# Score matmuls of a PEER layer: both parts of the activations in one wide pass

## The chip, the cores and the metric

One Trainium2 chip, one NeuronCore of it. The metric is the device time of one execution in microseconds: before the change the median of 3 runs is 2077.22 us (2074.89 to 2080.98). The rows below come from one profiled execution of 2076.17 us.

## The reference, cut to what matters

One transformer layer over 256 tokens of width 2048: a token mixer, a layer norm, and PEER channel mixing, which picks 16 experts per head (8 heads) out of 16384 and adds their outputs.

```
q = (xt @ w_pq).reshape(n_tok, 8, 2, 128)
scores = einsum('thcd,hckd->thck', q, sub_keys)
s_top, i_top = top_k(scores, 16)
cand = s_top[:, :, 0, :, None] + s_top[:, :, 1, None, :]      # 16 x 16 sums
best, pos = top_k(cand, 16)
expert_idx = ...;  gate = softmax(best)
u = take(expert_u, idx);  act = gelu(einsum('thkd,td->thk', u, xb))
v = take(expert_v, idx);  out = einsum('thk,thkd->td', gate * act, v)
x = layer_norm(alpha * x + out)
```

All is float32.

## The kernel before, in words

The kernel does not gather experts. It scores all 16384 experts against all tokens, applies Gelu, multiplies by a dense matrix of gates (zero where an expert isn't picked), and multiplies by all of expert_v.

A float32 product is made of three matmuls in fp32r: each operand is split into a high part (ScalarE copies it with rounding, `split_hi`) and a low part (the rest, by a subtraction, `split_lo`), and high x high, high x low and low x high are summed in PSUM (`three`, L399). `act_hi` and `act_lo` are the two parts of the activations, 16 row tiles of 256 tokens each.

The stages in order of time: the mixer's projections and heads (to about 500 us); the PEER query projection; from 564 us the **expert scores**, which the change touches; from about 1362 us the **values** (expert_v); the last layer norm.

The expert scores run over 128 tiles of 128 experts in 64 pairs. A pair has 8 steps q, four per tile (t = 0 for q 0 to 3, t = 1 for q 4 to 7), and a step has four row tiles (`score_pair`, L631). For every step:
- SyncE loads expert_u rows into `raw` (`u_half`), VectorE transposes two steps' worth at a time (`turn_u`, L1336), part A into `u_cols` in SBUF, part B into PSUM banks 4 to 7;
- ScalarE makes `split_hi` (`split_u`, L892); it waits until TensorE has freed the slot (four slots, `split_free`);
- GpSimd makes `split_lo` in part A (pairs 0 to 25, L1727), VectorE in part B (L1331);
- TensorE waits for `lo_ready`, and for the first step of a tile also for `score_free`, then does 4 x 3 matmuls of 256 columns, tile t into PSUM bank t.
When a tile is done, ScalarE's `gelu` (L898) reads it from PSUM and writes it to the tile's row of `wexp`, or, from tile LATE = 51 on, to the buffer `late`, which VectorE multiplies into a row that holds ones or gates (`late_tile`, L1440).

Beside the matmuls VectorE has other work, in an order written out by hand. Pairs 0 to 15 are the **search**: `rank_set` (L1395) finds the best 16 of a head's keys, with the four transpositions of the next pair between its steps. The **softmax start** (L1476) follows, then the **decode** (L1494), in 8 rounds that go with pairs 17 to 24 and do comparison, selection and sum in SBUF, again with the next pair's transpositions between. Pairs 28 to 59 are the **gate stage**: two groups of four tokens per pair, GpSimd (`distances`, `weigh`), ScalarE (`hot_rows`, L908), TensorE (`gates_after`, L656) and VectorE (`apply_gates`, L1446). Every engine works through its own list in order; semaphores join them, so a wait in one list holds all that stands behind it there. ScalarE's list in `u_pair` (L934) is: steps 4 to 7 of a pair, Gelu of its tile 0, steps 0 to 3 of the next pair, Gelu of tile 1.

## Time and profile before

| | us |
|---|---|
| runs, median of 3 | 2077.22 |
| profiled execution | 2076.17 |
| its span, first to last instruction | 2074.4 |
| TensorE busy | 2042.9 (98%) |
| VectorE busy | 1483.8 (72%) |
| ScalarE busy | 1130.9 (55%) |
| GpSimd busy | 546.5 (26%) |

The time outside the span is 1.8 us. Matmuls are pipelined: their busy times overlap, so the spacing of their starts is what tells their price. GpSimd's share is small over the span, but all of it lies between 200 and 1320 us.

### The profile page before, as it was taken

The numbers are of one execution on the slowest core, as the hardware profiler recorded it, in microseconds if no ns is written. First come the engines' busy times: TensorE is split into PE (matmuls) and PEld (weight loads), VectorE is DVE, ScalarE is ACT, GpSimd is POOL, SyncE is SP. The second block draws the span as 40 slices with busy tenths as digits, with TensorE's granted clock in tenths as the row PEclk, the third lists the DMA queues.
The fourth block names the chain that finished last, engine by engine and source line by source line (L and its number), as shares of the span: only waits on it lengthen the run. The fifth ranks groups of instructions, "written<-read, shape, count | busy, mean of one in ns | idle before, by whom it ended". The sixth has DMA issues, their size and how long they took to land.

```text
span 2074.4 us, 42390 instructions
## 1 busy us (share of the span) xinstructions
PE 2042.9 (98%) x12326; PEld 1827.3 (88%) x12326; DVE 1483.8 (72%) x2397; ACT 1130.9 (55%) x1956; POOL 546.5 (26%) x384
## 2 busy tenths in 40 slices
PE   8999999989999999999999999999999999999997
PEld 6888888778899999999999999987888888888886
DVE  4555776675588879799999999965555555555557
ACT  4455555445455555466666666555555555555553
POOL 0000330100189999944444444100000000000001
PEclk9999999999999999999999999999999999999999
DMA  7755554667586657555555555657755555555654
GB/s 246 228 173 172 172 164 141 229 166 206 162 203 184 182 157 194 169 163 156 159 159 156 159 156 158 172 192 227 214 193 193 192 194 192 195 192 192 193 193 152
DMA packets 254251, 378.48 MB, mean 182 GB/s; under 512 B 41859, under 2 KB 173059, under 8 KB 253571
## 3 DMA queue, kind: packets, MB, share of 16 engines
q1 hardware_dynamic: 254208, 377.98, 60.6%
q8 instruction: 21, 0.34, 0.1%
q14 instruction: 22, 0.16, 0.0%
HBM read 373.69 MB, written 4.19 MB: 182 GB/s over the span
## 4 chain that ended last, share of the span: by engine, by line
PE 82%; POOL 9%; DVE 3%; issue 3%; DMA 2%; SPq 1%; ACT 1%; POOLq 0%; DVEq 0%; ACTq 0%
PE ps L401 26%; PE ps L403 26%; PE ps L402 26%; POOL split_lo L1730 8%; PE ps L664 3%; DMA raw<-in_expert_v 1%; DVE split_lo L1070 1%; DMA raw<-in_w_out 0%; PE ps L396 0%; SPq L374 0%; ACT split_hi L740 0%; DMA x_nat<-in_x 0%; DVE end_lo L1596 0%; DVE stats L1606 0%; PE ps L611 0%
## 5 line engine op out<-in xcount | busy, mean ns | idle before, releaser
L1070 DVE TENSOR_TENSOR split_lo<-raw,split_hi 128x512 fp32r<-128x512 f32 x840 | 602.7, 720 | 493.7 <-ACT split_hi L740 492.6
L740 ACT ACTIVATE split_hi<-raw 128x512 fp32r<-128x512 f32 x840 | 528.9, 631 | 564.2 <-PE ps L403 547.4
L401 PE MATMUL ps<-act_hi,split_hi 128*128 128x256 f32 x2048 | 586.0, 286 | 0.8 <-POOL split_lo L1730 0.6
L403 PE MATMUL ps<-act_hi,split_lo 128*128 128x256 f32 x2048 | 579.3, 283 | 0.0
L402 PE MATMUL ps<-act_lo,split_hi 128*128 128x256 f32 x2048 | 579.3, 283 | 0.0
L401 PEld LDWEIGHTS ps<-act_hi,split_hi 128*128 128x128 f32 x2048 | 392.6, 192 | 2.6 <-POOL split_lo L1730 1.9
L402 PEld LDWEIGHTS ps<-act_lo,split_hi 128*128 128x128 f32 x2048 | 392.9, 192 | 0.0
L403 PEld LDWEIGHTS ps<-act_hi,split_lo 128*128 128x128 f32 x2048 | 392.6, 192 | 0.0
L401 PE MATMUL ps<-split_hi,whalf_hi 128*128 128x512 f32 x992 | 386.0, 389 | 1.4 <-DVE split_lo L1070 1.4
L402 PE MATMUL ps<-split_lo,whalf_hi 128*128 128x512 f32 x992 | 385.9, 389 | 0.0
L403 PE MATMUL ps<-split_hi,whalf_lo 128*128 128x512 f32 x992 | 385.9, 389 | 0.0
L1730 POOL TENSOR_TENSOR split_lo<-u_cols,split_hi 128x512 fp32r<-128x512 f32 x208 | 282.2, 1370 | 122.8 <-ACT split_hi L896 105.0
L401 PE MATMUL ps<-split_hi,act_hi 128*128 128x512 f32 x688 | 276.0, 401 | 6.0 <-DVE split_lo L1070 5.7
L896 ACT ACTIVATE split_hi<-ps 128x512 fp32r<-128x512 f32 x304 | 177.0, 593 | 173.4 <-PE ps L403 173.0
L403 PE MATMUL ps<-split_hi,act_lo 128*128 128x512 f32 x688 | 269.5, 392 | 0.0
L402 PE MATMUL ps<-split_lo,act_hi 128*128 128x512 f32 x688 | 269.0, 391 | 0.0
L1717 POOL TENSOR_TENSOR stats<-stats 128x1 f32<-128x1 f32 (+1 forms) x6 | 9.7, 1609 | 889.1 <-DVE stats L1612 749.1
L401 PEld LDWEIGHTS ps<-split_hi,whalf_hi 128*128 128x128 f32 x992 | 186.2, 188 | 40.5 <-DVE split_lo L1070 1.8
L403 PEld LDWEIGHTS ps<-split_hi,whalf_lo 128*128 128x128 f32 x992 | 186.2, 188 | 38.7
L402 PEld LDWEIGHTS ps<-split_lo,whalf_hi 128*128 128x128 f32 x992 | 186.2, 188 | 38.6
L1333 DVE TENSOR_TENSOR split_lo<-ps,split_hi 128x512 fp32r<-128x512 f32 x304 | 198.0, 678 | 25.6 <-ACT split_hi L896 20.4
L896 ACT ACTIVATE split_hi<-u_cols 128x512 fp32r<-128x512 f32 x208 | 131.2, 632 | 143.9 <-PE ps L403 142.6
(188 smaller groups left out, 2121.4 us busy)
## 6 DMA issues: line engine op xcount, KB each, us to landing
raw<-in_expert_u SPq DMA_DIRECT2D x1024, 128.0 KB, 2.9
raw<-in_expert_v SPq DMA_DIRECT2D x256, 512.0 KB, 4.7
raw<-in_w_in SPq DMA_DIRECT2D x112, 512.0 KB, 3.8
raw<-in_w_out SPq DMA_DIRECT2D x32, 512.0 KB, 3.9
raw<-in_w_pq SPq DMA_DIRECT2D x128, 128.0 KB, 2.9
cst<-in_tables SPq DMA_DIRECT2D x3, 768.0 KB, 5.3
x_nat<-in_x SPq DMA_DIRECT2D x4, 512.0 KB, 6.9
x_dram<-x_cols SPq DMA_DIRECT2D x1, 2048.0 KB, 8.0
```

The lines of the kernel that those rows point to most:

```text
L401: nc.tensor.matmul(acc, l_hi, r_hi, start=first, stop=False)
L402: nc.tensor.matmul(acc, l_hi, r_lo, start=False, stop=False)
L403: return nc.tensor.matmul(acc, l_lo, r_hi, start=False, stop=last)
L664: last = nc.tensor.matmul(ps[:, 2 + parity, i * P:(i + 1) * P], hot[:, parity, 1, i, :], hot[:, parity, 0, i, :], start=True, stop=True)
L740: nc.scalar.activation(split_hi[:, q % SPLITS, :], raw[:, q // 2, q % 2, :], ACT.Copy).then_inc(hi_ready, 1)
L896: nc.scalar.activation(split_hi[:, q % SPLITS, :], src, ACT.Copy).then_inc(hi_ready, 1)
L1070: vec.tensor_tensor(split_lo[:, q % SPLITS, :], raw[:, q // 2, q % 2, :], split_hi[:, q % SPLITS, :].bitcast(f32), ALU.subtract).then_inc( ...
L1333: vec.tensor_tensor(split_lo[:, q % SPLITS, :], ps[:, 4 + q % 4, :], split_hi[:, q % SPLITS, :].bitcast(f32), ALU.subtract).then_inc(lo_re ...
L1717: eng.tensor_tensor(stats[:, RSTD + first:RSTD + first + w], stats[:, VAR + first:VAR + first + w], stats[:, NHALF:NHALF + w], ALU.pow).th ...
L1730: eng.tensor_tensor(split_lo[:, q % SPLITS, :], u_cols[:, q // 2, q % 2, :], split_hi[:, q % SPLITS, :].bitcast(f32), ALU.subtract).then_i ...
```

## The change

`act_hi` and `act_lo` now lie side by side for each row tile (`act_both`). A step of the scores does four passes of 512 columns, `split_hi` against both parts at once, which wait for `hi_ready` alone, and then four of 256 columns, `split_lo` against `act_hi`, after `lo_ready` (in the last step of a tile one wide pass comes last). A tile's PSUM bank then holds two halves. ScalarE copies the second half to SBUF (`second_half_out`), VectorE adds it to the first half in PSUM (`add_halves`) and writes `wexp` or `late`, and ScalarE's Gelu now works there in place, later than before: for tile 0 after step 2 of the next pair, for tile 1 after step 6 of the next pair. In part A the tiles take four banks in turn; part B has two, as before. `late_tile` moves from VectorE to GpSimd. VectorE's sums stand at fixed places between the search's, the decode's and the splits' instructions. The loops of part A go over two pairs at a time. The core of the diff:

```diff
-        act_hi = at("act_hi", [KT, SEQ], f32r, A_HI)
-        act_lo = at("act_lo", [KT, SEQ], f32r, A_LO)
+        act_both = at("act_both", [KT, 2, SEQ], f32r, A_HI)
+        act_hi, act_lo = act_both[:, :, 0, :], act_both[:, :, 1, :]
+        halves = at("halves", [4, SEQ], f32, KEEP + 9216)
...
-            def score_pair(pair, after=None):
+            def score_pair(pair, after=None, parity=None):
+                first = 0 if parity is None else 2 * parity
+                def wide(bank, q, i):
+                    k = q % 4 * 4 + i
+                    return nc.tensor.matmul(ps[:, bank, :], split_hi[:, q % SPLITS, i * P:(i + 1) * P],
+                                            act_both[:, k, :, :].rearrange("p a t -> p (a t)"), start=k == 0,
+                                            stop=k == KT - 1)
                 for q in range(8):
-                    if q % 4 == 0:
-                        pe.wait_ge(score_free, pair * 2 + (q // 4 + 1))
+                    t, end = q // 4, q % 4 == 3
+                    if q % 4 == 0 and not (isinstance(pair, int) and pair < 2):
+                        pe.wait_ge(score_free, pair * 2 + (t + 1 if parity is None else t - 1))
+                    pe.wait_ge(hi_ready, pair * 8 + (Q_U + q + 1))
+                    wides = 3 if end else 4
+                    for i in range(wides):
+                        wide(first + t, q, i)
                     pe.wait_ge(lo_ready, pair * 8 + (Q_U + q + 1))
                     for i in range(4):
-                        last = three(ps[:, q // 4, 0:SEQ], split_hi[:, q % SPLITS, i * P:(i + 1) * P],
-                                     split_lo[:, q % SPLITS, i * P:(i + 1) * P], act_hi[:, q % 4 * 4 + i, :],
-                                     act_lo[:, q % 4 * 4 + i, :], q % 4 == 0 and i == 0, q % 4 == 3 and i == 3)
+                        k = q % 4 * 4 + i
+                        last = nc.tensor.matmul(ps[:, first + t, 0:SEQ], split_lo[:, q % SPLITS, i * P:(i + 1) * P],
+                                                act_hi[:, k, :], start=False, stop=False)
+                    if end:
+                        last = wide(first + t, q, 3)
...
+            def second_half_out(pair, t, parity=None):
+                bank = t if parity is None else 2 * parity + t
                 act.wait_ge(split_free, pair * 8 + (Q_U + SPLITS + 4 * t + 4))
-                if is_late:
+                if parity is None or isinstance(pair, int) and 2 * pair + t >= LATE:
                     act.wait_ge(late_used, pair * 2 + (t + 1 - LATE))
                     dst = late[:, t, :]
                 else:
+                    if not (isinstance(pair, int) and pair < 2):
+                        act.wait_ge(score_free, pair * 2 + (t - 1))
+                    dst = halves[:, bank, :]
+                nc.scalar.activation(dst, ps[:, bank, SEQ:2 * SEQ], ACT.Copy).then_inc(half_out, 1)
+            def gelu(pair, t, is_late):
+                act.wait_ge(score_free, pair * 2 + (t + 3))
...
-                nc.scalar.activation(dst, ps[:, t, 0:SEQ], ACT.Gelu).then_inc(score_free, 1)
+                nc.scalar.activation(dst, dst, ACT.Gelu).then_inc(gelu_done, 1)
...
                 for q in range(4, 8):
                     split_u(pair, q, part_a)
-                gelu(pair, 0, 0 in late_tiles)
+                    if q == 6 and not (isinstance(pair, int) and pair == 0):
+                        gelu(pair, -1, is_late)
+                second_half_out(pair, 0, parity)
...
                 for q in range(1, 4):
                     split_u(pair + 1, q, next_a)
-                gelu(pair, 1, 1 in late_tiles)
+                    if q == 2:
+                        gelu(pair, 0, is_late)
+                second_half_out(pair, 1, parity)
...
+            def add_halves(pair, t, bank=None):
+                n, t = (pair * 2 + t, t % 2)
+                if bank is None or isinstance(pair, int) and n >= LATE:
+                    dst = other = late[:, t, :]
+                else:
+                    dst, other = wexp[:, bass.ds(n, 1), :].rearrange("p a t -> p (a t)"), halves[:, bank, :]
+                dve.wait_ge(half_out, n + 1)
+                vec.tensor_tensor(dst, ps[:, t if bank is None else bank, 0:SEQ], other, ALU.add).then_inc(score_free, 1)
...
             for k in range(RAWS):
                 turn_u(SOFT + 1, k, True)
+                if k == 1:
+                    add_halves(SOFT, -1, 3)
+            add_halves(SOFT, 0, 0)
             softmax_start()
...
                 selected = [select(h) for h in range(2)]
                 turn_u(pair, 1, True)
+                add_halves(pair - 1, -1, 1 + 2 * s)
                 lc.until(selected[1])
                 collected = [collect(h) for h in range(2)]
                 turn_u(pair, 2, True)
                 turn_u(pair, 3, True)
+                add_halves(pair - 1, 0, 2 - 2 * s)
...
             split_turn(PAIRS - 1, 2, False)
-            late_tile(PAIRS - 1, -1)
             split_turn(PAIRS - 1, 3, False)
+            add_halves(PAIRS - 1, 0)
...
                     for q in range(3):
                         split(Q_V, q)
-            late_tile(PAIRS - 1, 0)
+            add_halves(PAIRS - 1, 1)
             split(Q_V, 3)
...
+                    def late_tile(pair, t, applied):
+                        pool.wait_ge(gelu_done, pair * 2 + (t + 1))
+                        if applied is not None:
+                            pool.wait_ge(gates_free, applied + 2)
+                        row = wexp[:, bass.ds(pair * 2 + t, 1), :].rearrange("p a t -> p (a t)")
+                        eng.tensor_tensor(row, row, late[:, t % 2, :], ALU.mult).then_inc(late_used, 1)
...
+                    weigh(0, 0)
                     with pool.Fori(0, GATES // 2 - 1) as i:
                         for s in range(2):
-                            weigh(i * 2 + s, s)
+                            weigh(i * 2 + (s + 1), 1 - s)
                             distances(i * 2 + (s + 2), s, True)
+                            late_tile(i + GATE0, s - 1, i * 2 + s)
```

In the search `rank_set` does `add_halves(n, -1, ...)` after the transposition of the next pair's steps 2 and 3, and `add_halves(n, 0, ...)` after that of its steps 6 and 7. In part B they stand after split_lo 4 and after the transposition that follows split_lo 7.

## Rows read from the trace of the kernel before

**Rows 1.** The page: busy time, share and instructions of each engine; chain by engine.
```profile
PE 2042.9 (98%) x12326; PEld 1827.3 (88%) x12326; DVE 1483.8 (72%) x2397; ACT 1130.9 (55%) x1956; POOL 546.5 (26%) x384
...
PE 82%; POOL 9%; DVE 3%; issue 3%; DMA 2%; SPq 1%; ACT 1%; POOLq 0%; DVEq 0%; ACTq 0%
```
**Rows 2.** Stretches: length, busy us (instructions) of PE, PEld, DVE, ACT, POOL; clock, DMA.
```profile
600.00:640.00 40.00, 40.00 (x336) 40.00 (x335) 32.87 (x102) 21.18 (x47) 36.22 (x28) 1.00 0.73 192
800.00:840.00 40.00, 39.36 (x320) 38.46 (x318) 35.83 (x35) 20.45 (x36) 39.30 (x27) 1.00 0.73 192
900.00:1300.00 400.00, 400.00 (x3373) 400.00 (x3372) 381.76 (x483) 270.85 (x422) 174.44 (x121) 1.00 0.54 158
1500.00:1600.00 100.00, 100.00 (x443) 82.81 (x442) 56.92 (x92) 52.14 (x92) 0.00 (x0) 1.00 0.59 193
```
**Rows 3.** Costliest groups: the score stage's first matmul; L402, L403 have 2048 each.
```profile
L401 PE MATMUL ps<-act_hi,split_hi 128*128 128x256 f32 x2048 | 586.0, 286 | 0.8 <-POOL split_lo L1730 0.6
```
**Rows 4.** Timeline of TensorE (start us, us, instruction), scores: first, last of 15.
```profile
1339.85 0.28 PE L401 MATMUL ps<-act_hi,split_hi 128*128 128x256 f32 x1
...
1341.53 0.28 PE L403 MATMUL ps<-act_hi,split_lo 128*128 128x256 f32 x1
```
**Rows 5.** Timeline of TensorE, query projection: first and last of 18 starts.
```profile
560.49 0.39 PE L401 MATMUL ps<-split_hi,act_hi 128*128 128x512 f32 x1
...
564.34 0.39 PE L403 MATMUL ps<-split_hi,act_lo 128*128 128x512 f32 x1
```
**Rows 6.** Timeline of ScalarE, search: the same split of two neighbouring pairs.
```profile
699.88 0.63 ACT L896 ACTIVATE split_hi<-u_cols 128x512 fp32r<-128x512 f32 x1 [0.81 <-PE ps L403]
...
711.40 0.63 ACT L896 ACTIVATE split_hi<-u_cols 128x512 fp32r<-128x512 f32 x1 [0.81 <-PE ps L403]
```
**Rows 7.** Instructions of single lines: duration ns min/median/max, first and last start.
```profile
L906 ACT ACTIVATE late<-ps x77: 376/378/384, 870.3 to 1365.3; 128x256 f32<-128x256 f32 x77
L1333 DVE TENSOR_TENSOR split_lo<-ps,split_hi x304: 666/676/693, 866.2 to 1360.2; 128x512 fp32r<-128x512 f32 x152
L1506 DVE TENSOR_TENSOR onehot<-onehot,idx_f x16: 642/662/1790, 770.1 to 849.1; 128x512 f32<-128x512 f32 x16
L1730 POOL TENSOR_TENSOR split_lo<-u_cols,split_hi x208: 1279/1301/1796, 561.5 to 864.8; 128x512 fp32r<-128x512 f32 x104
L1762 POOL TENSOR_TENSOR hot<-hot,picks_t x64: 1040/1041/1043, 891.9 to 1308.9; 128x512 f32<-128x512 f32 x64
```
**Rows 8.** Groups by line, 900 to 1300 us: count | busy us, mean ns.
```profile
L1444 DVE TENSOR_TENSOR wexp<-wexp,late 128x256 f32 x61 | 54.5, 894 | 0.0
```
**Rows 9.** Timeline of GpSimd in the decode; rows of a kind are merged.
```profile
770.12 3.48 POOL L1730 TENSOR_TENSOR split_lo<-u_cols,split_hi 128x512 fp32r<-128x512 f32 x2
...
785.44 2.56 POOL L1730 TENSOR_TENSOR split_lo<-u_cols,split_hi 128x512 fp32r<-128x512 f32 x2
...
811.09 54.98 POOL L1730 TENSOR_TENSOR split_lo<-u_cols,split_hi 128x512 fp32r<-128x512 f32 x38
```
**Rows 10.** Timeline of VectorE at the start of the decode.
```profile
759.66 1.25 DVE L1347 STREAM_TRANSPOSE u_cols<-raw 128x1024 f32<-128x1024 f32 x1 [1.64 <-POOL split_lo L1730]
...
770.09 2.35 DVE L1506 TENSOR_TENSOR onehot<-onehot,idx_f 128x512 f32<-128x512 f32 x2
772.37 1.23 DVE L1347 STREAM_TRANSPOSE u_cols<-raw 128x1024 f32<-128x1024 f32 x1
```
**Rows 11.** Timeline of ScalarE at the start of the decode.
```profile
757.54 0.64 ACT L896 ACTIVATE split_hi<-u_cols 128x512 fp32r<-128x512 f32 x1 [0.81 <-PE ps L403]
...
773.71 0.63 ACT L896 ACTIVATE split_hi<-u_cols 128x512 fp32r<-128x512 f32 x1 [1.20 <-DVE u_cols L1347]
```
**Rows 12.** Timeline of ScalarE, decode and start of part B.
```profile
816.35 0.63 ACT L896 ACTIVATE split_hi<-u_cols 128x512 fp32r<-128x512 f32 x1 [0.95 <-PE ps L403]
...
852.15 0.63 ACT L896 ACTIVATE split_hi<-u_cols 128x512 fp32r<-128x512 f32 x1 [0.96 <-PE ps L403]
...
869.76 0.60 ACT L896 ACTIVATE split_hi<-ps 128x512 fp32r<-128x512 f32 x1 [0.84 <-PE ps L403]
```

More of the change, by code:

```diff
@@ L667, in gates_after @@
                 return after
-            score_pair(0, rest_of_scores)
-            with pe.Fori(1, PICKS) as i:
-                score_pair(i)
-            score_pair(PICKS, picks_after)
+            score_pair(0, rest_of_scores, 0)
+            score_pair(1, parity=1)
+            with pe.Fori(1, PAIRS_A // 2) as i:
+                for s in range(2):
+                    score_pair(i * 2 + s, parity=s)
+            score_pair(PICKS, picks_after, parity=0)
             score_pair(PICKS + 1)
@@ L1415, in rank_set @@
                 turn_u(n + 1, 1, True)
+                if not (isinstance(n, int) and n == 0):
+                    add_halves(n, -1, 3 - 2 * s)
                 lc.until(low[1])
@@ L1429, in rank_set @@
                 turn_u(n + 1, 3, True)
+                add_halves(n, 0, 2 * s)
                 lc.until(second)
                 vec.max_index(head_p[:, s, 8:16], head_b[:, s, 8:16], rest[:, :]).then_inc(ranked, 1)
-            with dve.Fori(0, PH) as i:
+            lc = LoopChain(0, c0, TOP_STEPS)
+            for s in range(2):
+                rank_set(lc, s, s)
+            assert lc.n == TOP_STEPS, lc.n
+            with dve.Fori(1, PH) as i:
                 lc = LoopChain(i, c0, TOP_STEPS)
@@ L1493, in _, with decode @@
             c1 = chain.n
-            with dve.Fori(0, TB * PH // 2) as i:
-                lc = LoopChain(i, c1, DEC_STEPS)
-                pair = i + (SOFT + 2)
+            def decode(lc, m, s):
+                pair = m + (SOFT + 2)
                 def compare(h):
-                    row = pos_f[:, h, bass.ds(i * 2, 2), :].rearrange("p a k -> p (a k)")
+                    row = pos_f[:, h, bass.ds(m * 2, 2), :].rearrange("p a k -> p (a k)")
                     return lc.add(vec.tensor_tensor(onehot[h][:, :, :], row.unsqueeze(2).to_broadcast([P, 2 * TOPK, TOPK]),
@@ L1522, in _ @@
                 turn_u(pair, 3, True)
+                add_halves(pair - 1, 0, 2 - 2 * s)
                 lc.until(collected[1])
-                assert lc.n == DEC_STEPS
+            with dve.Fori(0, TB * PH // 4) as i:
+                lc = LoopChain(i, c1, 2 * DEC_STEPS)
+                for s in range(2):
+                    decode(lc, i * 2 + s, s)
+                assert lc.n == 2 * DEC_STEPS
             chain.n += TB * PH // 2 * DEC_STEPS
```

82 lines of the change are left out of this document (47 added, 35 removed).

## The prediction

> **What bounds the kernel now.** I read the page first. TensorE is busy for 98% of the span, and 82% of the chain that ended last runs on it; 9% runs on GpSimd, whose only work in that chain is split_lo [rows 1]. Then a table of stretches, to see whether another engine is close behind. In the search (600 to 640 us) TensorE never rests and GpSimd is at 36.2 of 40 us; in the decode (800 to 840) GpSimd is at 39.3 and TensorE starts 320 matmuls where it started 336; in the gate stage (900 to 1300) TensorE never rests and VectorE is at 381.8 of 400 [rows 2]. So one engine bounds nearly all of it, but each part has a second one within 10%: a gain on TensorE is worth only what those leave.
>
> The changed stage is 64 pairs of 128-expert tiles. Each pair is 8 steps, a step is 4 row tiles, and each of these is now three matmuls of 256 columns, 6144 in all [rows 3]. A busy time is no use for their price, since they overlap (0.28 us each in the rows); starts are. Fifteen starts in a row, 1339.85 to 1341.53, give 0.1200 us from one to the next [rows 4]. For 512 columns, 443 starts in 100 us of the value stage give 0.2257 [rows 2], and the 18 starts from 560.49 to 564.34 give 0.2265 [rows 5]. Twice the columns cost 1.88 times as much: about 13 ns of each matmul do not depend on its columns. A step is 12 x 0.1200 = 1.440 us. ScalarE's first split of two neighbouring pairs starts at 699.88 and 711.40, 11.52 us apart, which is 8 x 1.440: in the search nothing but TensorE sets the pace [rows 6].
>
> **The matmuls.** Three instructions become two: 0.3600 us becomes 0.2257 + 0.1200 = 0.3457, or 0.3465 with the other price. I take the middle, 0.3460: a step is 1.384 us, 0.056 less. Times 512 steps: 28.7 us (27.6 to 29.3). Both parts then write one bank, so the halves must be added afterwards. The wide passes wait for hi_ready alone and the low ones for lo_ready, one more wait per step; today's one wait per step leaves no gap in the starts, and I price the second at nothing. If it did show, the least it could cost is nothing and the most one uncovered pass, 0.28 - 0.12 = 0.16 us, in the steps where split_lo comes late. As the wide passes go first, split_lo may come 0.9 us later than now.
>
> The Trainium skill speaks against this step ("TensorE: Matmul & The Clock Gate", section "Wait — 56ns, not 53.3ns?"): back-to-back matmuls are spaced by columns over 2.4 GHz and some 2.5 ns. By that rule a dropped instruction gives 2.5 ns, and 2048 of them 5.1 us instead of 28.7. The trace does not agree: it has 13.3 ns over 256 columns and 12.4 over 512, with a weight load before each, and the trace decides.
>
> **ScalarE.** Per tile it now does a copy of the second half from PSUM and a Gelu in SBUF where it did one Gelu from PSUM. Such an instruction takes 0.38 us [rows 7]; one more per tile is 0.76 us in a pair. It is at 270.9 of 400 us where it is fullest [rows 2], so the time itself hides. Its order does not: the Gelu of a tile stands behind split 6 (or split 2) and waits for VectorE's sum. Behind it in ScalarE's queue stand the next split_hi, then split_lo, then TensorE.
>
> **VectorE.** Two sums of 256 columns per pair, one operand in PSUM. A 512-column one of that kind takes 0.68 us and 0.666 to 0.693 over 304 of them, many beside GpSimd work [rows 7]; 256 columns fewer should leave about 0.40. The bounds are 0.34 (half) and 1.79, the longest two-operand instruction in the trace, which had both operands in SBUF beside GpSimd [rows 7]. I take 0.40, since the operand in PSUM is what the steady row shares with it.
> In the search VectorE has 32.9 of 40 us, 9.5 of 11.52 per pair; with 0.8 it has 10.3 of 11.07. The sums fit. The late Gelu's wait there: the sum of the older tile follows the transposition that starts when split_lo 3 is done, so it ends 1.2 + 0.3 (that transposition runs late) + 0.4 = 1.9 us after it. Split_lo 3 ends 2.0 us after split_hi 3 starts (0.63 + 1.30 and the signals), split_hi 6 ends 3 x 1.384 + 0.63 = 4.8 after it, so 2.8 us after the same event. No wait, by 0.9 us.
> In the gate stage a pair takes 13.28 us (96 + 16 matmuls, 3373 in 400 us [rows 2]), of which the 16 gate matmuls are 1.76. VectorE has 12.7 of that. It loses two multiplications by the late tile, 1.8 us per pair (61 of 0.894 in 400 us [rows 8]), and gains 0.8: 11.7 of the new 12.83. This stage gets its full gain.
>
> **GpSimd.** Its split_lo is 1.30 us, and with work waiting two take 2.56, so it can go every 1.28 us; it must go every 1.384. Fine, except beside the decode: there two take 3.48, so 1.74 each [rows 9]. In the gate stage it takes over the late multiplications, two per pair. For 512 columns from SBUF it needs 1.04 to 1.30 us [rows 7], so 0.5 to 0.7 each. It has 174 of 400 us; 6.6 of 12.8 per pair after. It does its weigh one step earlier in the order, so the gate matmuls don't wait for it.
>
> **The start of the decode** is where I expect a new wait. The softmax start and the first decode round keep VectorE without rest from 759.66 to 773.54 (end of the transposition that starts at 772.37) [rows 10]; it is late already now, for ScalarE waits for that transposition until 773.71 [rows 11]. After the change the sum of tile 33 stands behind it. ScalarE's split_hi 7 of pair 16 starts at 757.54 [rows 11]; from there, split_hi 6 of pair 17 is 7 steps on, 767.2 to 767.9. Then comes the Gelu of tile 33. VectorE's stretch gets 0.34 longer by the sum of tile 32, but ScalarE's stop lets GpSimd run dry, and then the two selections, 2.35 us from 770.09 [rows 10], lose their slowdown (0.64 each at the least [rows 7]), 1.1 us; with the sum itself it is done at 773.54 + 0.34 - 1.1 + 0.4, about 773.2. Gelu, then split_hi 7 from 773.6 to 774.2 (5.0 us late), split_lo until 775.6. TensorE ends step 6 at 772.7 and would end step 7 at 774.1; now it ends at 775.6 + 4 x 0.12 + 0.226 = 776.3. That is 2.2 us lost, and the lead of split_lo is gone.
> **The rest of the decode** runs at GpSimd's pace: 11.93 us a pair from 816.35 to 852.15 (three pairs) [rows 12], which a faster TensorE doesn't change. From its last split_lo of pair 17, GpSimd needs 94.2 us for the other 64 (771.9 to 866.1 [rows 9]), about 1 us less at the end, where it now waits for TensorE's pace. 775.6 + 93.2 = 868.8, plus 0.7 us: TensorE ends pair 25 at 869.5. Today that is at 869.7 (ScalarE's split that waits for it starts at 869.76 [rows 12]). So these 76 steps (from step 3 of pair 16) gain nothing, where they should have gained 4.3 us. Of that I count 2.2 for the new wait, the rest for GpSimd.
>
> **The end.** The last sum stands behind three split_lo of the value stage. TensorE needs it after its first six value matmuls, 1.36 us after the last score matmul; copy and sum are done 0.95 us after it. Nothing.
>
> **Sum.** 28.7 - 4.3 = 24.4 us. The profiled execution takes 2076.17 us, so 2051.8; it lies 1.05 under the median of the runs, 2077.22, so **2052.8**.
>
> **The rivals.**
> 1. *Hidden wait doesn't bite.* VectorE reaches the sum of tile 33 earlier or split_lo's extra 0.9 us carries over it, and the decode gains too. For it: the wide passes need no split_lo. Against: 5 us of delay is more than any lead. All 28.7: 2048.5.
> 2. *The decode round closes a ring.* In every decode pair: transposition 1.17, sum, comparison some 2.3 as the selection, transposition, selection 2.3, transposition, sum, Gelu 0.38, split_hi 0.63, split_lo 1.3 and back, 11.5 us with sums of 0.4. That is under 11.93. If the sums collide with GpSimd as the late multiplications do (0.894 [rows 8], up to twice that), it is 12.5 to 14; at 13.0 eight pairs lose 8.6 us: 2061.4.
> 3. *The change doesn't do what it says.* The gap between matmuls follows the columns in this mix (a narrow pass behind a wide one pays for its weight load), so wide and narrow are 0.36 us as before, or nearly. Against: both 512-column rows. Gain 5 us at best: 2072. The skill's rule named above would end in this case.
> 4. *VectorE becomes the bound of the gate stage: slower.* It decides once a sum costs over (12.83 - 12.7 + 1.8) / 2 = 0.97 us. At the longest row, 1.79, VectorE needs 14.5 us per pair against 12.83: 32 x 1.65 = 53 us, so 2106. For it: VectorE is at 95% there today, and GpSimd gets two more SBUF multiplications. Against: the operand in PSUM, and 304 steady rows.
>
> **How the numbers follow.** Chances: forecast 0.58, rival 1 0.11, rival 2 0.14, rival 3 0.08, rival 4 0.09. Faster by over 0.3% (6.2 us, about what these runs can tell from none) is under 2071.0: the forecast and rivals 1 and 2, 0.83. Same: 0.08. Slower: 0.09. The range takes in rivals 1 and 2, with the scatter of the runs before (2.3 below the median, 3.8 above): 2046 to 2065.
>
> **What would show it.** Right: 512 and 256-column starts 0.226 and 0.120 apart; 11.07 us a pair in the search and 12.83 in the gate stage; VectorE's sums at 0.40 with little spread; VectorE's share falling in the gate stage; one ScalarE stop of 5 us in pair 17, ended by a sum; the decode still at 11.9 a pair. Wrong: sums of 0.8 us and more, more than one such stop, a gap at the new wait for lo_ready in each step, or a pair of the gate stage over 13 us.

## The result, and the profile after

| | before | after |
|---|---|---|
| median of the compared runs, us | 2076.05 (4 runs) | 2063.35 (2061.88 to 2064.2, 4 runs) |
| profiled execution, us | 2076.17 | 2063.09 |

The ratio is 0.9927, with a 95% interval of 0.9916 to 0.9939: faster by 0.73%, more than the 0.3% that can be told from nothing. The forecast was 2052.8 in a range of 2046 to 2065. So the sign was right and the time lies in the range, near its slow end, which had been set by a rival (the decode's ring, 2061.4, and the scatter of the runs) and not by the sum. 10.5 us of the gain are missing, and the rest of this section finds where.

The page of the kernel after: busy time, then the two kinds of score matmul (busy us, mean ns, idle before). They answer to [rows 1, 3].
```profile
PE 2026.2 (98%) x10278; PEld 1716.1 (83%) x10278; DVE 1491.4 (72%) x2448; ACT 1167.3 (57%) x2084; POOL 600.7 (29%) x461
...
L640 PE MATMUL ps<-act_both,split_hi 128*128 128x512 f32 x2048 | 565.3, 397 | 2.2 <-ACT split_hi L915 2.2
...
L655 PE MATMUL ps<-act_both,split_lo 128*128 128x256 f32 x2048 | 327.2, 282 | 0.7 <-POOL split_lo L1788 0.4
```
The 2048 matmuls fewer are there. The idle time of 2.2 us in front of L640 is the only long stop in the whole stage, and ScalarE ended it. Waits that are shorter than the overlap of the matmuls don't show as idle time; they show in the spacing of the starts.

First the stage is cut at ScalarE's splits: each one from the fifth on needs a slot that TensorE has freed, and the two single ones at which the parts meet were released by TensorE (the brackets). The kernel after: duration, first and last start of the split line; then two single starts from ScalarE's timeline.
```profile
L915 ACT ACTIVATE split_hi<-ps x304: 575/597/606, 865.6 to 1346.8; 128x512 fp32r<-128x512 f32 x152
L915 ACT ACTIVATE split_hi<-u_cols x208: 612/632/636, 562.6 to 864.2; 128x512 fp32r<-128x512 f32 x104
```
```profile
754.23 0.63 ACT L915 ACTIVATE split_hi<-u_cols 128x512 fp32r<-128x512 f32 x1 [0.46 <-PE ps L640]
...
869.82 0.60 ACT L915 ACTIVATE split_hi<-ps 128x512 fp32r<-128x512 f32 x1 [0.51 <-PE ps L640]
```
The same of the kernel before:
```profile
L896 ACT ACTIVATE split_hi<-ps x304: 577/597/600, 865.4 to 1359.6; 128x512 fp32r<-128x512 f32 x152
L896 ACT ACTIVATE split_hi<-u_cols x208: 614/632/635, 560.7 to 864.0; 128x512 fp32r<-128x512 f32 x104
```
With 757.54 [rows 11] and 869.76 [rows 12] for the two single starts, the stage falls into three parts (us):

| | steps | before | after | difference | forecast |
|---|---|---|---|---|---|
| search, to split 7 of pair 16 | 135 | 196.8 | 191.6 | -5.2 | -7.6 |
| decode stretch, to split 3 of pair 26 | 76 | 112.2 | 115.6 | +3.4 | 0 |
| the rest, to the last split | 300 | 489.8 | 477.0 | -12.8 | -16.8 |

The forecast column is 0.056 us by the steps, less the 4.3 us that the prediction gave back in the decode. Ahead of the stage the execution after is 1.9 us later (562.6 for 560.7), and behind it 0.4 us shorter. Nothing there is changed but where the two parts of the activations lie; over the executions of this study the stage starts between 560.6 and 564.9, so I take the 1.9 as scatter.

**TensorE's pace.** The timeline of TensorE after, in the search (equal rows are merged; start, us, instruction):
```profile
700.74 1.09 PE L640 MATMUL ps<-act_both,split_hi 128*128 128x512 f32 x4
701.67 0.63 PE L655 MATMUL ps<-act_both,split_lo 128*128 128x256 f32 x4
702.14 0.86 PE L640 MATMUL ps<-act_both,split_hi 128*128 128x512 f32 x3
```
From start to start four wide passes take 0.93 us, 0.2325 each, and four narrow ones 0.47, 0.1175 each: a step of 1.40 us (the rows are given to 0.01 us, so each price is good to some 0.002). Over 112 steps of the search, split by split, it is 1.4014. The forecast had 1.384, with 0.2257 to 0.2265 for the wide pass.

**The decode.** What ScalarE waited for from 760 to 870 us, after (us in total, times, longest):
```profile
ACT wexp L937 <- DVE wexp L1399: 38.6, 16, 6.1
```
The forecast had one such wait of 5 us; there are 16 with 38.6 us. The timeline of ScalarE after, its Gelus alone (the wait before each in brackets):
```profile
770.80 0.42 ACT L937 ACTIVATE wexp<-wexp 128x256 f32<-128x256 f32 x1 [6.14 <-DVE wexp L1399]
...
774.73 0.42 ACT L937 ACTIVATE wexp<-wexp 128x256 f32<-128x256 f32 x1 [1.16 <-DVE wexp L1399]
...
831.02 0.42 ACT L937 ACTIVATE wexp<-wexp  x1 [3.89 <-DVE wexp L1399]
...
843.13 0.42 ACT L937 ACTIVATE wexp<-wexp  x1 [3.88 <-DVE wexp L1399]
```
The last two are 12.11 us apart: that is the round now, where it was 11.93 [rows 12]. Every second Gelu holds up the next split in ScalarE's queue by almost 4 us, the others by 1.2 to 1.3. VectorE after, in one such round (its sum is the 0.38 at the end):
```profile
774.61 3.24 DVE L1550 TENSOR_TENSOR onehot<-pos_f,small 128x512 f32<-128x512 f32 x2
777.77 1.23 DVE L1387 STREAM_TRANSPOSE u_cols<-raw 128x1024 f32<-128x1024 f32 x1
778.93 2.35 DVE L1556 TENSOR_TENSOR onehot<-onehot,idx_f 128x512 f32<-128x512 f32 x2
781.21 1.23 DVE L1387 STREAM_TRANSPOSE u_cols<-raw 128x1024 f32<-128x1024 f32 x1
782.37 0.38 DVE L1399 TENSOR_TENSOR wexp<-ps,halves 128x256 f32 x1
```
In front of the sum stand a comparison of 3.24 us for two and a selection of 2.35. How the round closes, by single rows of VectorE, then of GpSimd, after:
```profile
833.38 1.25 DVE L1387 STREAM_TRANSPOSE u_cols<-raw 128x1024 f32<-128x1024 f32 x1 [0.17 <-POOL split_lo L1788]
...
832.04 11.89 POOL L1788 TENSOR_TENSOR split_lo<-u_cols,split_hi 128x512 fp32r<-128x512 f32 x8 [0.22 <-ACT split_hi L915]
```
A transposition waits for GpSimd's split_lo; sum, comparisons, transposition, selections, transposition and sum follow it on VectorE without a gap; the Gelu waits for that sum, split_hi stands behind the Gelu, and split_lo waits for split_hi. That is a closed ring of 12.11 us. GpSimd's eight split_lo take 11.89 of them, so its own pace is close behind. Where the first wait ends, TensorE after looks like this:
```profile
768.91 0.63 PE L655 MATMUL ps<-act_both,split_lo 128*128 128x256 f32 x4
771.79 1.65 PE L640 MATMUL ps<-act_both,split_hi 128*128 128x512 f32 x3 [2.25 <-ACT split_hi L915]
773.24 1.14 PE L655 MATMUL ps<-act_both,split_lo 128*128 128x256 f32 x4
774.18 1.78 PE L640 MATMUL ps<-act_both,split_hi 128*128 128x512 f32 x5
...
776.28 1.09 PE L640 MATMUL ps<-act_both,split_hi 128*128 128x512 f32 x4
```
It stood still for 2.25 us, and that isn't all: from the start at 771.79 to that of the next full step, at 776.28, two steps take 4.49 us instead of 2.80. The table of stretches after shows why (length, busy us of PE, PEld, DVE, ACT, POOL; granted clock, DMA share, GB/s):
```profile
770.00:772.00 2.00, 0.21 (x1) 0.21 (x2) 2.00 (x5) 1.20 (x4) 0.18 (x1) 0.94 0.73 223
772.00:774.00 2.00, 2.00 (x7) 1.47 (x8) 1.97 (x2) 1.57 (x4) 2.00 (x2) 0.50 0.71 195
774.00:776.00 2.00, 2.00 (x9) 1.68 (x9) 2.00 (x3) 1.21 (x3) 2.00 (x3) 0.70 0.68 151
```
Behind the pause the granted clock is 0.50, the lower level of 1.2 GHz; with means of 0.94 in the stretch before and 0.70 in the one after, it was low from about 771.8 to 775.2. Half speed for 3.4 us is the 1.7 us, so TensorE comes out of this place 4.0 us late, 2.25 by the pause and 1.7 by the clock. From ScalarE's split 3 of pair 17 to that of pair 18 it is 15.2 us for the 11.21 of a search pair.

Not all of this reaches the time. GpSimd, then TensorE, after:
```profile
771.82 31.23 POOL L1788 TENSOR_TENSOR split_lo<-u_cols,split_hi 128x512 fp32r<-128x512 f32 x21 [5.39 <-ACT split_hi L915]
```
```profile
805.41 0.74 PE L655 MATMUL ps<-act_both,split_lo 128*128 128x256 f32 x4 [0.41 <-POOL split_lo L1788]
```
GpSimd starts again at 771.82, released by ScalarE, and then works for 31 us without a wait. TensorE is held by it: from 791.07 to 857.75 the narrow passes start late in about half of the steps, at 805.41 by enough to show as idle time. A TensorE at full clock would have come to that wait 1.7 us earlier and waited longer. So by these rows what the first stop costs the stretch is GpSimd's stop, and the 1.7 us of the clock are covered; no run took away the drop of the clock alone.

Pair by pair (split 3 to split 3) pair 17 takes 3.7 us more than in the kernel before, the seven behind it 1.0 together, and pair 25 1.2 less.

**The gate stage.** Table of stretches, 900 to 1300 us, after; then the two lines that are new in it, and two ScalarE splits of neighbouring pairs.
```profile
900.00:1300.00 400.00, 400.00 (x2472) 357.18 (x2471) 369.12 (x495) 296.97 (x494) 221.77 (x184) 1.00 0.56 162
```
```profile
L1399 DVE TENSOR_TENSOR late<-ps,late 128x256 f32<-128x256 f32 x62 | 25.2, 407 | 0.0
...
L1797 POOL TENSOR_TENSOR wexp<-wexp,late 128x256 f32 x61 | 45.3, 743 | 5.6 <-ACT late L937 5.6
```
```profile
1001.60 0.60 ACT L915 ACTIVATE split_hi<-ps 128x512 fp32r<-128x512 f32 x1 [1.20 <-PE ps L655]
...
1014.55 0.60 ACT L915 ACTIVATE split_hi<-ps 128x512 fp32r<-128x512 f32 x1 [1.20 <-PE ps L655]
```
TensorE never rests, VectorE falls from 381.8 [rows 2] to 369.1, a sum costs 0.407. A pair takes 12.95 us (12.96 over 28 of them, 13.29 before), 0.12 to 0.13 over the 12.83 of the forecast; eight steps that are 0.0174 us longer than forecast would be 0.14.

### The profile page after: what moved, and what is told of

It is laid out like the page before. It is cut to its first block, busy times and chain, and to the rows that moved or that the text cites. A ratio compares the mean times of both kernels' runs of the same rounds, so it can differ in the third digit from the quotient of the medians.

```text
span 2061.3 us, 38813 instructions
## 1 busy us (share of the span) xinstructions
PE 2026.2 (98%) x10278; PEld 1716.1 (83%) x10278; DVE 1491.4 (72%) x2448; ACT 1167.3 (57%) x2084; POOL 600.7 (29%) x461
## 4 chain that ended last, share of the span: by engine, by line
PE 81%; POOL 8%; DVE 4%; issue 3%; DMA 1%; ACT 1%; SPq 1%; POOLq 0%; DVEq 0%; ACTq 0%
PE ps L404 18%; PE ps L406 18%; PE ps L405 18%; PE ps L640 14%; POOL split_lo L1788 8%; PE ps L655 7%; PE ps L682 3%; PE ps L399 1%; DMA raw<-in_expert_v 1%; DVE onehot L1550 1%; DMA raw<-in_w_out 0%; DVE split_lo L1110 0%; SPq L377 0%; DVE onehot L1556 0%; ACT split_hi L759 0%
## 5 line engine op out<-in xcount | busy, mean ns | idle before, releaser
L640 PE MATMUL ps<-act_both,split_hi 128*128 128x512 f32 x2048 | 565.3, 397 | 2.2 <-ACT split_hi L915 2.2
L640 PEld LDWEIGHTS ps<-act_both,split_hi 128*128 128x128 f32 x2048 | 351.1, 189 | 48.2 <-ACT split_hi L915 2.5
L655 PEld LDWEIGHTS ps<-act_both,split_lo 128*128 128x128 f32 x2048 | 311.4, 189 | 50.9 <-POOL split_lo L1788 9.1
L655 PE MATMUL ps<-act_both,split_lo 128*128 128x256 f32 x2048 | 327.2, 282 | 0.7 <-POOL split_lo L1788 0.4
L1788 POOL TENSOR_TENSOR split_lo<-u_cols,split_hi 128x512 fp32r<-128x512 f32 x208 | 281.0, 1363 | 124.9 <-ACT split_hi L915 111.3
L404 PE MATMUL ps<-split_hi,act_both 128*128 128x512 f32 x688 | 275.5, 400 | 6.3 <-DVE split_lo L1110 6.1
L406 PE MATMUL ps<-split_hi,act_both 128*128 128x512 f32 x688 | 269.5, 392 | 0.0
L405 PE MATMUL ps<-split_lo,act_both 128*128 128x512 f32 x688 | 268.8, 391 | 0.0
L1373 DVE TENSOR_TENSOR split_lo<-ps,split_hi 128x512 fp32r<-128x512 f32 x304 | 205.8, 681 | 30.1 <-ACT split_hi L915 30.0
L406 PEld LDWEIGHTS ps<-split_hi,whalf_lo 128*128 128x128 f32 x992 | 186.2, 188 | 38.6
L1387 DVE STREAM_TRANSPOSE ps<-raw 128x1024 f32<-128x1024 f32 x152 | 191.4, 1260 | 5.8
L404 PEld LDWEIGHTS ps<-split_hi,act_both 128*128 128x128 f32 x688 | 130.0, 189 | 33.1 <-DVE split_lo L1110 5.9
```

Source lines behind the costliest of these rows:

```text
L404: nc.tensor.matmul(acc, l_hi, r_hi, start=first, stop=False)
L405: nc.tensor.matmul(acc, l_hi, r_lo, start=False, stop=False)
L406: return nc.tensor.matmul(acc, l_lo, r_hi, start=False, stop=last)
L640: return nc.tensor.matmul(ps[:, bank, :], split_hi[:, q % SPLITS, i * P:(i + 1) * P], act_both[:, k, :, :].rearrange("p a t -> p (a t)"), ...
L655: last = nc.tensor.matmul(ps[:, first + t, 0:SEQ], split_lo[:, q % SPLITS, i * P:(i + 1) * P], act_hi[:, k, :], start=False, stop=False)
L1373: vec.tensor_tensor(split_lo[:, q % SPLITS, :], ps[:, 4 + q % 4, :], split_hi[:, q % SPLITS, :].bitcast(f32), ALU.subtract).then_inc(lo_re ...
```

## The experiments

Two questions were open: why a wide pass costs 0.2325 us here, and which part of the change costs the decode 3.4 us. "Step" is the mean of 112 steps in the search, "stretch" the 76 steps of the decode; both are from ScalarE's splits in the one profiled execution. The times are medians, the ratios are against runs of the kernel before on the same chip. The chips differ, so ratios compare better than times.

| | time, us | ratio (interval) | step, us | stretch, us |
|---|---|---|---|---|
| before | 2076.05 | | 1.4405 | 112.2 |
| after | 2063.35 | 0.9927 (0.9916 to 0.9939) | 1.4014 | 115.6 |
| later Gelus | 2060.54 | 0.9914 (0.99 to 0.9928) | 1.4014 | 111.3 |
| turned steps | 2064.75 | 0.9933 (0.9919 to 0.9947) | 1.3972 | 117.1 |
| alternating | 2069.26 | 0.996 (0.9944 to 0.9975) | 1.4139 | 116.5 |
| wide as two | 2078.44 | 1.0002 (0.9992 to 1.0011) | 1.4322 | 116.0 |
| later Gelus + PSUM one-hot | 2055.5 | 0.9893 (0.9876 to 0.991) | 1.4014 | 106.5 |
| all three | 2053.17 | 0.9874 (0.9857 to 0.989) | 1.3972 | 106.9 |
| before + PSUM one-hot | 2075.52 | 0.9986 (0.9976 to 0.9996) | 1.4405 | 110.0 |
| all wide (more work) | 2268.65 | one run | 1.8139 | 137.8 |
| after + PSUM one-hot | 2055.91 | 0.9902 (0.9885 to 0.9918) | 1.4014 | 108.1 |

**Later Gelus.** The Gelus of part A stand one tile later in ScalarE's order.
```diff
-                        gelu(pair, -1, is_late)
+                        gelu(pair, -2 if part_a else -1, is_late)
...
-                    if q == 2:
-                        gelu(pair, 0, is_late)
+                    if q == 2 and not (isinstance(pair, int) and pair == 0):
+                        gelu(pair, -1 if part_a else 0, is_late)
...
+            gelu(PAIRS_A - 1, 0, False)
```


> Only the place of the Gelus of part A in ScalarE's order is changed: each is done one tile (four steps) later, so the sum it waits for is long done. Changed kernel: ScalarE waits 38.6 us for VectorE's sums in the decode, in 16 waits, and the stretch from split_hi 7 of pair 16 to split_hi 3 of pair 26 takes 115.6 us (112.2 before). Theory A (the Gelu's wait in ScalarE's order costs the decode): the stretch falls to about 112, GpSimd's pace of 11.9 us a pair, total 3 to 4 us less, 2059.5. Rival B (VectorE's longer list and GpSimd's slowed subtractions set the decode, 12.1 us a pair, whatever ScalarE does): the waits go but the stretch stays within 1 us of 115.6, total within 1 us of 2063.35.

ScalarE's waits for sums are gone, and what it waits for from 760 to 870 us is TensorE, and VectorE's transpositions:
```profile
ACT split_hi L915 <- PE ps L655: 29.2, 39, 1.1
ACT split_hi L915 <- DVE u_cols L1388: 13.5, 9, 2.3
```
The stretch is 4.3 us shorter, pair 17 takes 11.5 us where it took 15.2, and the granted clock stays at 1.00 (the row below). So the Gelu's place costs the stretch 4.3 us, most of it in pair 17. It is GpSimd's stop that goes: its last split_lo of pair 17 ends 4.9 us earlier (counted from split 7 of pair 16), and the 64 behind it take 0.7 us longer. The times alone don't show the gain, since the interval overlaps that of the changed kernel; the stretch does. The other pairs settle at 11.9 us, not at 11.2: VectorE and GpSimd are now both without rest.
```profile
760.00:800.00 40.00, 39.34 (x221) 33.40 (x219) 39.69 (x42) 23.00 (x44) 37.48 (x27) 1.00 0.57 146
800.00:840.00 40.00, 39.77 (x214) 31.81 (x215) 40.00 (x42) 20.81 (x41) 40.00 (x27) 1.00 0.72 183
```

**Turned steps.** Odd steps take their narrow passes first, so that runs of eight equal passes follow each other.
```diff
+                    if q % 2 == 1:
+                        pe.wait_ge(lo_ready, pair * 8 + (Q_U + q + 1))
+                        narrows()
                     for i in range(4):
                         last = wide(first + t, q, i)
+                    if q % 2 == 0:
+                        pe.wait_ge(lo_ready, pair * 8 + (Q_U + q + 1))
+                        last = narrows()
```


> Only the order of matmuls in a step is changed: even steps wide then narrow, odd steps narrow then wide, so narrow follows narrow and wide follows wide across steps: 4 changes between the two kinds per tile instead of 8. In the changed kernel a step takes 1.4005 us, 0.0145 more than 4 x 0.2265 + 4 x 0.1200. Theory S (the excess comes with the changes of kind, about 7 ns each): a step falls to 1.393, the stage by 3.7 us less what odd steps lose by needing split_lo first, total about 2060. Rival P (a wide pass over act_both simply costs 0.2325): step stays 1.400, total 2063 or a little more.

The step is 1.3972, between 1.393 and 1.400, and the time is not better: the search gains 0.5 us and the decode stretch loses 1.5. TensorE's stop at the start of the decode is 3.76 us there, for 2.25, and split_lo ended it, which an odd step now needs first.

**Alternating.** Wide and narrow take turns within a step.
```diff
-                        last = nc.tensor.matmul(... split_lo ..., act_hi[:, k, :], ...)
+                            wide(first + t, q, i)
+                            last = narrow()
```


> The other direction: wide and narrow in turn for each row tile, 8 changes of kind per step where there were 2, and a step needs split_lo from its start. Theory S (7 ns per change): a step takes 1.386 + 8 x 0.00725 = 1.444, the stage 22 us longer, total about 2085. Rival P (price belongs to the wide pass): step stays 1.400, total 2063 to 2065.

The timeline of TensorE, alternating, search:
```profile
699.94 0.40 PE L640 MATMUL ps<-act_both,split_hi 128*128 128x512 f32 x1
700.17 0.28 PE L652 MATMUL ps<-act_both,split_lo 128*128 128x256 f32 x1
700.29 0.40 PE L640 MATMUL ps<-act_both,split_hi 128*128 128x512 f32 x1
```
A wide and a narrow pass together take 0.35 us in this row, 0.3535 by the step of 1.4139; in the changed kernel they take 0.3504, with turned steps 0.3493, and at the two separate prices 0.3465. The order matters, but not in proportion to the changes between the widths: alternating has nearly four times those of the changed kernel (30 a tile for 8) and not quite twice its excess (7.0 ns a pair for 3.9), turning has half and still three quarters of it (2.8). Both numbers lie between what the two theories gave, so neither is confirmed by them. Alternating makes the time longer, 0.996 for 0.9927.

**All wide.** The narrow passes are 512 columns as well, which adds the product of the two low parts.
```diff
-                        last = nc.tensor.matmul(ps[:, first + t, 0:SEQ], ..., act_hi[:, k, :], ...)
+                        last = nc.tensor.matmul(ps[:, first + t, :], ..., act_both[:, k, :, :].rearrange("p a t -> p (a t)"), ...)
```


> The changed kernel with the four narrow passes of each step 512 columns wide as well, over both activation parts (this adds the product of the two low parts, which the kernel leaves out otherwise): eight passes of 512 columns in a step and none of 256. It tells why a wide pass takes 0.2328 us in the search and 0.2265 in the value stage. Theory M (the excess comes with the change between 512 and 256 columns): all passes take 0.2265 to 0.2270, a step 1.81 to 1.82 us. Theory O (a 512-column pass over this operand, at an address order of its own, costs 0.2325 wherever it stands): a step of 1.86 us. The time would be 2063 + 512 x 0.41 = 2273 us by M, 2298 by O.

The timeline of TensorE, all wide:
```profile
700.87 1.07 PE L655 MATMUL ps<-act_both,split_lo 128*128 128x512 f32 x4
701.77 1.07 PE L640 MATMUL ps<-act_both,split_hi 128*128 128x512 f32 x4
```
Four passes in 0.90 us, eight in 1.81 (1.8139 over the search), 0.2267 each, and 2268.65 us for the whole where one theory had 2273 and the other 2298. A wide pass over this operand has the price of [rows 5]; it is dearer only among narrow ones. What in TensorE makes it so stays open: weight loads that overlap differently would be one reading, but no run here separates it.

**Wide as two.** 14 of 16 wide passes are made of two with 256 columns; banks, copies, sums and Gelus stay as changed.
```diff
+                    for a in (1, 0):
+                        last = nc.tensor.matmul(ps[:, bank, a * SEQ:(a + 1) * SEQ],
+                                                split_hi[:, q % SPLITS, i * P:(i + 1) * P],
+                                                act_both[:, k, a, :], start=False, stop=False)
```


> Everything of the change stays (halves, sums, later Gelus, four banks), but 14 of the 16 wide passes of each tile are made of two passes of 256 columns. Here the matmul gain is gone and what the other parts cost stands alone. If they cost only what the decode showed (about 6 us against a gain of 20.2): 3 x 0.1200 in 14 of 16 row tiles gives 17.7 us more than the changed kernel, about 2080, 4 to 5 us over before. Rival (the other parts cost nothing once TensorE is slower, since the decode is paced by GpSimd anyway): about 2075 to 2076.

This takes most of the gain out and leaves the price. The step is 1.432, still 0.0083 under that of the kernel before (two passes of a tile are wide), which is 4.2 us over 512 steps; the stretch is 3.75 us longer than before, and the time is that of the kernel before (1.0002), neither the 4 to 5 us more of the one expectation nor without a price as in the rival. The search takes 195.7 us for 196.8 and a gate pair 13.23 for 13.29. So what the halves are seen to cost is in the decode; neither the search nor the gate stage pays for them.

**The one-hot array in PSUM.** Comparison, selection and sum of the decode work in two unused banks, so that comparison and selection have one operand in SBUF instead of two.
```diff
+            onehot_ps = [ps[:, 4 + h, :].rearrange("p (a k) -> p a k", k=TOPK) for h in range(2)]
+            chain.step(vec.tensor_copy(ps[:, 6, 0:TOPK], iota[:, 0:TOPK]))
...
-                    return lc.add(vec.tensor_tensor(onehot[h][:, :, :], row.unsqueeze(2).to_broadcast([P, 2 * TOPK, TOPK]),
-                                                    iota[:, 0:TOPK].unsqueeze(1).to_broadcast([P, 2 * TOPK, TOPK]),
+                    return lc.add(vec.tensor_tensor(onehot_ps[h], row.unsqueeze(2).to_broadcast([P, 2 * TOPK, TOPK]),
+                                                    ps[:, 6, 0:TOPK].unsqueeze(1).to_broadcast([P, 2 * TOPK, TOPK]),
```
On top of the later Gelus:

> On top of the Gelus that run one tile later, the decode's one-hot array lies in the unused banks 4 and 5 of PSUM and its iota in bank 6, so that the comparison and the selection have one operand in SBUF instead of two. Theory G (with ScalarE's wait gone, the decode pairs go at the pace of GpSimd's three operations per pair, 11.9 us, and these are slow because VectorE's operations with two operands from SBUF run beside them): GpSimd's operations get shorter, the decode pairs fall from 11.9 us to 11.2, the pace of the search, the stretch from 111.3 us to about 106.5, and the time is some 5 us under that of the later Gelus alone (about 2055 where that one had 2060). Rival N (the decode pace comes from ScalarE or the order of waits, or the comparison isn't what slows GpSimd): decode pairs stay at 11.9 us, time within 1 us of the later Gelus alone.

Groups by line from 760 to 865 us, first in the kernel after (count, busy us, mean ns):
```profile
L1788 POOL TENSOR_TENSOR split_lo<-u_cols,split_hi 128x512 fp32r<-128x512 f32 x68 | 98.9, 1490 | 7.2 <-ACT split_hi L915 6.7
...
L1550 DVE TENSOR_TENSOR onehot<-pos_f,small 128x512 f32<-128x512 f32 x16 | 25.8, 1653 | 0.3 <-DVE pos_f L1531 0.3
L1556 DVE TENSOR_TENSOR onehot<-onehot,idx_f 128x512 f32<-128x512 f32 x16 | 16.6, 1074 | 0.0
```
and with the later Gelus and the one-hot in PSUM:
```profile
L1791 POOL TENSOR_TENSOR split_lo<-u_cols,split_hi 128x512 fp32r<-128x512 f32 x68 | 87.5, 1301 | 7.6 <-ACT split_hi L915 2.6
...
L1553 DVE TENSOR_TENSOR ps<-pos_f,ps 128x512 f32<-128x512 f32 x16 | 10.3, 689 | 0.3 <-DVE ps L1544 0.3
L1559 DVE TENSOR_TENSOR ps<-ps,idx_f 128x512 f32<-128x512 f32 x16 | 10.1, 679 | 0.0
```
The comparison falls from 1.65 to 0.69 us, the selection from 1.07 to 0.68, and GpSimd's split from 1.49 to 1.30. The stretch is 106.5 us, which is 76 steps at 1.4014: nothing but TensorE sets the pace any more. That GpSimd's work is what slows VectorE, and not the place of the operands by itself, the kernel after shows too: its first two selections, both operands in SBUF, take 1.25 us while GpSimd stands still (768.06 to 769.31), and the next two 2.35 beside it. This is the collision that the Trainium skill tells of ("SBUF — State Buffer", section "Who interferes with whom": a VectorE instruction with two SBUF inputs contends with a GpSimd one that reads SBUF, one with at most one, outside the 2-port modes, doesn't); these rows agree, on both engines. The edit moves the outputs to PSUM as well as an input; which of the two frees the engines was not separated.

On the kernel before, alone:

> The kernel before with nothing changed but the one-hot array and the iota of the decode in PSUM banks that it doesn't use. It has no wait of ScalarE for sums. Theory G: its decode pairs, 11.8 to 12.4 us, fall to about the 11.55 of its late pairs, the decode stretch from 112.2 us to about 109.4, time 2.8 us less (ratio 0.9987). Rival N: stretch within 0.5 us of 112.2, ratio 1.000.

The stretch fell from 112.2 to 110.0, where 109.4 was expected, and the ratio is 0.9986 for 0.9987. The kernel before lost 2.2 us by this collision; the changed one lost more (the next experiment).

On the kernel after, alone:

> The changed kernel with the one-hot array and the iota of the decode in unused PSUM banks, and the Gelus left where they are. It tells whether ScalarE's repeated wait for sums in the decode comes from the order alone or from the slow comparison and selection ahead of each sum. Theory R (VectorE's round is too long because its comparison takes 1.6 us and its selection 1.1 beside GpSimd): at 0.68 us each, the sum of the first decode pair is done 1.7 us earlier (two comparisons 1.4 us instead of 3.1), ScalarE's first wait falls from 6.1 us to 4.4, TensorE idles 0.5 us instead of 2.25 and keeps its clock, the later waits end no step late, decode pairs are at 11.2 us, the stretch is at 106.5 to 108 us and the time at 2055 to 2057. Rival O (the Gelu behind split 6 and 2 makes ScalarE wait whatever the comparison costs): decode pairs stay over 11.8 us and the stretch over 112 us, time 2060 or more.

What ScalarE waited for from 760 to 870 us in this kernel, and its first Gelu in the decode:
```profile
ACT wexp L937 <- DVE wexp L1399: 7.9, 5, 4.5
```
```profile
767.56 0.42 ACT L937 ACTIVATE wexp<-wexp 128x256 f32<-128x256 f32 x1 [4.51 <-DVE wexp L1399]
```
and TensorE there:
```profile
768.55 0.96 PE L640 MATMUL ps<-act_both,split_hi 128*128 128x512 f32 x3 [0.62 <-ACT split_hi L915]
769.92 0.74 PE L655 MATMUL ps<-act_both,split_lo 128*128 128x256 f32 x4 [0.41 <-POOL split_lo L1790]
```
The waits of 38.6 us are 7.9, and the wait of 6.1 us is 4.5; TensorE stands still for 0.62 and 0.41 us, and the granted clock from 760 to 800 us is 1.00. The stretch is 108.1 us. So it isn't the Gelu's place alone that makes ScalarE wait in every round, but also the slow comparison and selection ahead of the sum. With these in PSUM, 1.6 us are left for the Gelu's place in the stretch (108.1 against 106.5), where it was 4.3 with them in SBUF.

**All three.** Later Gelus, PSUM one-hot, turned steps.

> The later Gelus, the one-hot in PSUM, and odd steps that take their four narrow passes ahead of the wide ones. If the three gains add: step 1.397 us instead of 1.401, which over 512 steps is 2 us, so about 2053 us beside 2055 for the same without the turned steps. In a kernel with the turned steps alone the decode stretch was 117 us; if that was the Gelu wait alone it goes here as well, and the stretch is at 106 us. Rival: the turned steps ask for the high split of the next step later and the low one earlier, which makes a new wait in the decode, and the time is not under that of the kernel without them.

Its time, 2053.17, is the lowest, but the intervals of this kernel and of the one without turned steps overlap, and the profiled stages have the same length: 775.1 us from the first to the last split without, 775.2 with them (562.3 to 1337.5). The steps gain 0.5 us in the search; a gate pair takes 12.97 us for 12.96, and the stretch 0.4 us more. That turned steps pay is not shown. What is shown is that the changed kernel with the one-hot in PSUM, with or without later Gelus, beats both kernels: 0.9893 with them; 0.9902 without, where the interval (to 0.9918) just touches that of the changed kernel (from 0.9916) and the stretch is 7.5 us shorter.

## Why the prediction was right in its sign and 10.5 us too fast

The range held, but partly by luck: its slow end came from a rival with sums that collide, which didn't happen, and the largest miss, the price of the wide pass, had been given 1.1 us of room only (27.6 for 28.7). By its own steps, in the order in which it took them:
- **The price of the matmuls: mechanism right, size wrong.** It held that dropped instructions give back what doesn't depend on columns, about 13 ns each, and took the wide pass from two stretches in which all passes are wide. In the mix of four and four it costs 0.2325, not 0.226, and a step 1.4014, not 1.384. In the search that is the 2.4 us of the 9.8 that the stage missed. In the rest 300 steps would miss 5.2 us by it; 4.0 are missing, since pairs 26 and 27 and the gate matmuls gave some back (a gate pair gained 0.33 us where eight steps gain 0.31). Together 6.4 us. The rival that let a narrow pass pay for its weight load behind a wide one had the direction of the error, but it took away all but 5 us of the gain. The Trainium skill's rule of a fixed 2.5 ns per matmul ("TensorE: Matmul & The Clock Gate", section "Wait — 56ns, not 53.3ns?") would have given 5.1 us; by the step of 1.4014 the passes gave 512 x 0.0391 = 20.0 us, 9.8 ns for each of the 2048 dropped.
- **The wait for lo_ready: right.** It costs nothing in the search, whose steps are the sum of their passes; in the decode it is where TensorE is held by GpSimd.
- **VectorE's sums: right.** 0.38 to 0.42 us, steady in all three parts; the rival in which they cost 1 us and more and bound the gate stage is dead.
- **The gate stage: right but for the matmul price.** VectorE fell to 369 of 400 us, and the stage got the full gain of its steps. GpSimd's late multiplication takes 0.74 us where 0.5 to 0.7 was worked out, and TensorE rests for none of it.
- **The start of the decode: right place, too small.** The wait was 6.1 us where 5.0 was worked out (the sum was done 16.5 us after split 7 of pair 16, not 15.7). One small instruction ahead of it makes up for the difference, the softmax start's copy of 16 columns (L1526, L1479 before): 1.25 us for 0.20. It began 0.07 us behind the start of one of GpSimd's split_lo and ended 0.03 behind its end; the same holds, to 0.02 us, in all seven runs in which it took 1.25 us; in the kernel before it began near the end of one, and in the run with wide as two, begun 0.02 behind the start, it took 0.15. That it was held by that instruction is read from these times and was not tested by a run. TensorE's pause was 2.25 us where a loss of 2.2 was worked out; the 1.7 us at the lower clock behind it were not thought of, but were covered.
- **The rest of the decode: wrong.** The prediction said that GpSimd's pace of 11.93 us stands whatever TensorE does, and that the ring of comparison, transposition, selection, sum, Gelu, split closes in 11.5. GpSimd's pace did stand, at 11.89 us of work a round; the ring didn't close as said. It read the comparison as costing what the selection costs, 2.3 us for two; it costs 3.24, and the ring is 12.1. (The terms that it lists add up to 11.2, not 11.5; with the comparisons 0.9 us longer they give the 12.1.) The kernel before already had 1.32 us a comparison, 2.65 for two, in its groups by line (mean ns behind the busy us):
```profile
L1500 DVE TENSOR_TENSOR onehot<-pos_f,small 128x512 f32<-128x512 f32 x16 | 20.6, 1324 | 0.3 <-DVE pos_f L1484 0.3
```
This is the rival of the ring, with another cause than it gave (the comparison, not the sum) and a small part of its size. The stretch is 115.6 us, not 112.2: 3.4 of the 9.8. In the prediction's own sum: GpSimd's last split_lo of pair 17 ended 18.9 us after split 7 of pair 16, at 773.10, where 18.1 was worked out; the other 64 took 94.6 us for 93.2; and from there, 867.69, to split 3 of pair 26 it was 2.1 us for 1.0. So the late start is 0.8 of the 3.4, and the slower rounds and the end behind them are 1.4 and 1.2.

6.4 and 3.4 are the 9.8 us that the stage missed. The profiled execution took 2063.09 us against 2051.8: the other 1.5 are the later start of the stage less its shorter tail.

## What to carry to other kernels

Price an instruction in the mix in which it will stand: the wide pass cost 0.2267 us among wide ones and 0.2325 among narrow ones, and that was most of the missing gain. Before a queue gets a new wait, read the longest instruction ahead of what it waits for, at the durations it has beside the other engine. Behind a pause of TensorE ask which engine sets the pace: here the low clock cost TensorE 1.7 us, and GpSimd's pace covered them. And where VectorE and GpSimd work side by side, put what VectorE works on into an unused PSUM bank, so that one operand is left in SBUF: that took 7.5 us off the decode of the changed kernel, about half of what the change itself brought.

## What had not been expected of the hardware

- Passes of 512 and 256 columns in turn cost more than each among its own: 0.3504 us a pair in runs of four, 0.3535 alternating, against 0.2265 + 0.1200. With 512 alone it is 0.2267.
- A pause of TensorE of 2.25 us was followed by a granted clock of 0.50 for about 3.4 us, which cost TensorE another 1.7 us; pauses of 0.62 and 0.41 us, 1.0 us apart, were not.
- A copy of 16 columns by VectorE took 1.25 us when it began 0.07 us behind the start of a split_lo of GpSimd, and ended 0.03 us behind it; in the kernel before, begun near the end of one, it took 0.20.
- VectorE's comparison with two operands in SBUF took 1.65 us beside GpSimd's work and 0.69 with one of them in PSUM; GpSimd's own instruction went from 1.49 to 1.30 us.
